# Modulation columns in pairs of chunks, two row tiles by 1024 columns to a slot

## The reference

```python
c_act = jax.nn.silu(c)
for l in range(DEPTH):                       # DEPTH = 2
    mod = c_act @ w_mod[l] + b_mod[l]        # w_mod[l]: 2048 x 6144
    shift, scale, gate = jnp.split(mod, 3, axis=-1)
    h = rmsnorm(x, norm_gain[l]) * (1.0 + scale[:, None, :]) + shift[:, None, :]
    proj = h @ w_in[l]                       # 2048 x 7504
    ...                                      # attention, retention, gates -> y_a, y_b
    y = jnp.concatenate([y_a, y_b], axis=-1) @ w_out[l]
    x = x + gate[:, None, :] * y
```

## Time and profile before

| | |
|---|---|
| median of three runs | 1870.87 us (1869.70 to 1872.94) |
| profiled execution | 1869.93 us |
| its span | 1868.1 us, 25006 instructions |
| TensorE busy | 1826.4 us (98%), granted clock 0.993 |
| VectorE busy | 1351.8 us (72%) |
| ScalarE busy | 990.8 us (53%) |
| split, L1859 | 721.1 us in 580 instructions |
| pieces, L1989 | 110.9 us in 154 and 52.3 us in 70 instructions |
| HBM read | 418.45 MB |

### The profile page before, as it was taken

One profiled execution on the slowest core, in us unless ns is written; L12 is line 12 of the kernel. 1 busy time (PEld: TensorE's weight loads), 2 busy tenths in 40 slices (PEclk: granted clock), 3 DMA queues, 4 the chain that ended last, 5 costly groups with the idle time before them and its releaser, 6 DMA issues.

```text
span 1868.1 us, 25006 instructions
## 1 busy us (share of the span) xinstructions
PE 1826.4 (98%) x9520; PEld 1512.4 (81%) x9520; DVE 1351.8 (72%) x1949; ACT 990.8 (53%) x1359; POOL 203.0 (11%) x256
## 2 busy tenths in 40 slices
PE   5989999999999999999999999999999999999997
PEld 3768788889888878888888888888888888888886
DVE  6979999988987778857765544488885466665555
ACT  6664455446447445544654644476765445444464
POOL 0000002100000000210000000044441020031001
PEclk9989999999999999999999999999999999999999
DMA  9989978965986986744365555554555555557562
GB/s 350 373 323 343 332 232 302 322 224 182 330 297 229 361 280 225 235 159 159 124 225 185 182 199 192 191 181 161 177 178 182 185 191 184 184 180 248 182 197 94
DMA packets 211826, 424.07 MB, mean 227 GB/s; under 512 B 7680, under 2 KB 12684, under 8 KB 210316
## 3 DMA queue, kind: packets, MB, share of 16 engines
q1 hardware_dynamic: 209788, 414.94, 65.6%
q10 hardware_dynamic: 1936, 7.76, 1.0%
HBM read 418.45 MB, written 4.21 MB: 226 GB/s over the span
## 4 chain that ended last, share of the span: by engine, by line
PE 91%; DMA 3%; DVE 2%; ACT 2%; issue 1%; SPq 0%; DVEq 0%; POOLq 0%; POOL 0%; ACTq 0%
PE acc L684 28%; PE acc L686 28%; PE acc L685 28%; DMA raw<-in_w_in 2%; DVE scr L2078 1%; DMA raw<-in_w_mod 1%; PE tps L725 1%; PE tps L765 1%; ACT w_hi L1418 0%; ACT proj L1393 0%; PE sps L996 0%; PE tps L988 0%; PE sps L952 0%; PE sps L893 0%; PE sps L892 0%
## 5 line engine op out<-in xcount | busy, mean ns | idle before, releaser
L1859 DVE TENSOR_TENSOR w_lo<-raw,w_hi 128x1024 fp32r<-128x1024 f32 (+1 forms) x580 | 721.1, 1249 | 444.8 <-ACT w_hi L1246 442.5
L1246 ACT ACTIVATE w_hi<-raw 128x1024 fp32r<-128x1024 f32 (+1 forms) x580 | 606.1, 1050 | 762.3 <-PE acc L686 684.3
L684 PE MATMUL acc<-w_hi,ht_hi 128*128 128x512 f32 (+1 forms) x2304 | 910.5, 395 | 0.5 <-issue 0.4
L686 PE MATMUL acc<-w_hi,ht_lo 128*128 128x512 f32 (+1 forms) x2304 | 894.2, 388 | 0.0
L685 PE MATMUL acc<-w_lo,ht_hi 128*128 128x512 f32 (+1 forms) x2304 | 892.3, 387 | 0.0
L686 PEld LDWEIGHTS acc<-w_hi,ht_lo 128*128 128x128 f32 x2304 | 432.4, 188 | 90.3
L684 PEld LDWEIGHTS acc<-w_hi,ht_hi 128*128 128x128 f32 x2304 | 432.9, 188 | 87.4 <-issue 3.2
L685 PEld LDWEIGHTS acc<-w_lo,ht_hi 128*128 128x128 f32 x2304 | 433.3, 188 | 83.4
L1989 DVE SCALAR_TENSOR_TENSOR scr<-raw,vcol,scr 128x512 f32<-128x512 f32 x154 | 110.9, 761 | 4.8 <-issue 0.4
L2078 DVE SCALAR_TENSOR_TENSOR scr<-raw,vcol,scr 128x1024 f32<-128x1024 f32 x56 | 68.0, 1278 | 6.6 <-DMA raw<-in_w_mod 6.6
L1989 DVE SCALAR_TENSOR_TENSOR proj<-raw,vcol,proj 128x512 f32<-128x512 f32 x70 | 52.3, 788 | 1.9
(11 more groups left out here) (305 smaller groups left out, 1446.8 us busy)
## 6 DMA issues: line engine op xcount, KB each, us to landing
raw<-in_w_in SPq DMA_DIRECT2D x208, 1024.0 KB, 5.1
raw<-in_w_mod SPq DMA_DIRECT2D x64, 1024.0 KB, 6.2
raw<-in_w_mod SPq DMA_DIRECT2D x64, 512.0 KB, 6.3
raw<-in_w_out SPq DMA_DIRECT2D x32, 1024.0 KB, 5.2
raw<-in_w_o SPq DMA_DIRECT2D x16, 1024.0 KB, 5.2
raw<-in_w_ple_gate SPq DMA_DIRECT2D x16, 1024.0 KB, 5.1
raw<-in_w_b_out SPq DMA_DIRECT2D x8, 1024.0 KB, 5.1
raw<-in_w_a_out SPq DMA_DIRECT2D x8, 1024.0 KB, 5.1
```

Source lines behind the costliest of these rows:

```text
L684: pe.matmul(o, hi_m, w_hi[:, slot, u, 0:width], start=start, stop=False)
L686: mm = pe.matmul(o, lo_m, w_hi[:, slot, u, 0:width], start=False, stop=stop)
L1246: act.activation(w_hi[:, x % SPL, :, 0:width], raw[:, j, 2 * (x % halves):2 * (x % halves) + 2, 0:width], ACT.Copy).then_inc(hi_ready, 1)
L1859: dve.tensor_tensor(w_lo[:, x % SPL, :, 0:width], raw[:, j, 2 * (x % halves):2 * (x % halves) + 2, 0:width], w_hi[:, x % SPL, :, 0:width]. ...
```

## The change

Behind the front, modulation chunks are made in pairs. A slot holds two row tiles by 1024 columns instead of four by 512, still 1 MB. A pair has eight pieces instead of two times four. Each piece is two instructions of 1024 columns into one accumulator of 1024; the closing addition is gone, and a wait and a semaphore increment of VectorE stand in its place. Both instructions of a piece now depend on the one before. TensorE adds up a pair in one group of eight narrow matmuls, and VectorE takes eight columns at once.

The pieces of layer 0 start one chunk later. The four of chunk 2 are gone; chunk 6 has four instead of two and chunk 7 has two (behind halves 5 and 7) where it had none. The other chunks keep their places. With this the gate's columns of layer 0 are complete later: their sum is behind half (6, 7) and their take behind the split of (7, 3). TensorE's turning of the gate's columns goes from (6, 4) to (7, 1), ScalarE's copy of them from half 8 to half 13 of chunks 6 and 7, and the DMA that writes them out from half 9 to half 14.

```diff
-PIECES = [{2: FULL, 3: FULL, 4: FULL, 5: FULL, 6: (1, 3), 8: (1, 3, 7), 9: FULL, 10: FULL, 11: (1, 3, 5),
+PIECES = [{3: FULL, 4: FULL, 5: FULL, 6: FULL, 7: (5, 7), 8: (1, 3, 7), 9: FULL, 10: FULL, 11: (1, 3, 5),
...
-                            mods[2 * j + 1] = piece // 4, piece % 4, item % RAW
+                            mods[2 * j + 1] = piece // 8, piece % 8, item % RAW
...
-                    if q == 3:
+                    if q == 7:
                         SUM_AT[n], TAKE_AT[n] = (l, k, 7), (l, k + 1, 3)
...
-            if 12 <= n < 16 or n == 23:
-                return macc_h[:, (n + n // 23) % 2, :, :]
-            return macc[:, n % 2, :, :]
+            return (macc_h if n in (6, 7, 11) else macc)[:, n % 2, :, :]
...
+            def land_pair(slot, src):
+                sp.wait_ge(raw_read, free.next(2))
+                sp.dma_start(raw[:, slot, :, :].rearrange("p (k a) n -> p k (a n)", a=2), src).then_inc(raw_landed[slot], 16)
...
-                            land(slot, full(wm[n // 12])(q, n % 12 * CH, CH))
+                            land_pair(slot, wm[n // 6][:, 2 * q:2 * q + 2, n % 6 * 2 * CH:(n % 6 + 1) * 2 * CH])
...
-            def mod_sums(src, parts=1):
+            def mod_sums(src):
                 pe.wait_ge(mod_taken, m_taken.next())
-                if parts == 1:
-                    pe.wait_ge(mod_ready, m_ready.next())
-                for j in range(4):
-                    for e in range(parts):
-                        mm = pe.matmul(tps[:, 1, j:j + 1], src[:, e, j * P:(j + 1) * P], ones,
-                                       start=e == 0, stop=e == parts - 1)
-                mm.then_inc(mod_summed, 1)
+                m_taken.skip(1)
+                pe.wait_ge(mod_ready, m_ready.next())
+                for e in range(2):
+                    for j in range(4):
+                        mm = pe.matmul(tps[:, 1, 4 * e + j:4 * e + j + 1], src[:, e, j * P:(j + 1) * P], ones,
+                                       start=True, stop=True)
+                mm.then_inc(mod_summed, 2)
...
-                if x == 4 and l == 0:
+                if x == 9 and l == 0:
                     gate_columns(l)
...
-            def mod_piece(to, q, slot, one_sum=False):
-
+            def mod_piece(n, q, slot):
+
+                to = home(n)
                 if q == 0:
-                    dve.wait_ge(mod_summed, m_free.next())
+                    dve.wait_ge(mod_summed, max(2 + 8, 2 * n))
                 dve.wait_ge(raw_landed[slot], m_land[slot].next(16))
                 for u in range(2):
-                    if q or u:
+                    src, c_col = raw[:, slot, 2 * u:2 * u + 2, :], v2("c", 2 * q + u)
+                    if q == 0 and u == 0:
+                        r = dve.tensor_scalar(to, src, c_col, None, ALU.mult)
+                    else:
                         dve.wait_ge(raw_read, own.ahead(0))
-                    for e in range(2):
...
+                        r = dve.scalar_tensor_tensor(to, src, c_col, to, ALU.mult, ALU.add)
                     r.then_inc(raw_read, 1)
                     own.skip(1)
-                if q == 3 and one_sum:
+                if q == 7:
                     dve.wait_ge(raw_read, own.ahead(0))
-                    dve.tensor_tensor(to[:, 0, :], to[:, 0, :], to[:, 1, :], ALU.add).then_inc(mod_ready, 1)
+                    dve.sem_inc(mod_ready, 1)
```

More of the change, by code:

```diff
@@ L87 @@
 FULL = (1, 3, 5, 7)
-PIECES = [{2: FULL, 3: FULL, 4: FULL, 5: FULL, 6: (1, 3), 8: (1, 3, 7), 9: FULL, 10: FULL, 11: (1, 3, 5),
+PIECES = [{3: FULL, 4: FULL, 5: FULL, 6: FULL, 7: (5, 7), 8: (1, 3, 7), 9: FULL, 10: FULL, 11: (1, 3, 5),
            12: (5, 7), 13: (3, 7), 15: (1, 3), 16: FULL, 17: FULL, 18: (1, 3)},
           {1: (3, 7), 2: (1, 3, 7), 3: (1, 3, 7), 4: (1, 5), 5: (1, 5), 6: (1, 3), 8: (1, 3)}]
+FRONT = 2
 RAW = 4
@@ L481, in slots_of_chunks @@
         def slots_of_chunks():
-            plan, item, piece = [{}, {}], 0, 4 * 8
+            plan, item, piece = [{}, {}], 0, 8 * 4
             for l in range(DEPTH):
-                for k in range(0 if l else 2, NCH + 5):
+                for k in range(0 if l else FRONT, NCH + 5):
                     rows, mods = [], {}
@@ L491, in slots_of_chunks @@
                         if 2 * j + 1 in PIECES[l].get(k, ()):
-                            mods[2 * j + 1] = piece // 4, piece % 4, item % RAW
+                            mods[2 * j + 1] = piece // 8, piece % 8, item % RAW
                             item, piece = item + 1, piece + 1
                     plan[l][k] = rows, mods
-                assert item % RAW == 0 and piece % 4 == 0
+                assert item % RAW == 0 and piece % 8 == 0
             return plan
@@ L1527, in norms @@
                         index_relu()
+                    if x == 13 and l == 0:
+                        gate_columns()
                     if x == 4 or x == 13:
@@ L1533, in norms @@
                                        ACT.Sqrt, bias=eps, scale=1.0 / HD).then_inc(root_ready, 1)
-                    if x == 8 and l == 0:
-                        gate_columns()
                     if x == 9:
-                        if l == 0:
-                            gates_out(l)
                         act.wait_ge(acc_taken, first_acc + 5)
@@ L1541, in norms @@
                     if x == 14:
+                        if l == 0:
+                            gates_out(l)
                         act.wait_ge(k_turned, ktn.next())
@@ L1873, in body @@
                             n, q, slot = mods[x % 8]
-                            mod_piece(home(n), q, slot, one_sum=True)
+                            mod_piece(n, q, slot)
                         if evac and x % group == min(3, group - 1) and not (first and x < group):
@@ L1974, in _, with mod_take @@
             own = Seen(dve, raw_read, 8)
-            def mod_piece(to, q, slot, one_sum=False):
+            def mod_piece(n, q, slot):
+                to = home(n)
                 if q == 0:
-                    dve.wait_ge(mod_summed, m_free.next())
+                    dve.wait_ge(mod_summed, max(2 + 8, 2 * n))
                 dve.wait_ge(raw_landed[slot], m_land[slot].next(16))
                 for u in range(2):
-                    if q or u:
+                    src, c_col = raw[:, slot, 2 * u:2 * u + 2, :], v2("c", 2 * q + u)
+                    if q == 0 and u == 0:
+                        r = dve.tensor_scalar(to, src, c_col, None, ALU.mult)
+                    else:
                         dve.wait_ge(raw_read, own.ahead(0))
-                    for e in range(2):
[L1985 to L1990, removed]
+                        r = dve.scalar_tensor_tensor(to, src, c_col, to, ALU.mult, ALU.add)
                     r.then_inc(raw_read, 1)
                     own.skip(1)
-                if q == 3 and one_sum:
+                if q == 7:
                     dve.wait_ge(raw_read, own.ahead(0))
-                    dve.tensor_tensor(to[:, 0, :], to[:, 0, :], to[:, 1, :], ALU.add).then_inc(mod_ready, 1)
[L1997 to L2001, removed]
+                    dve.sem_inc(mod_ready, 1)
+            def mod_take(n):
+                dve.wait_ge(mod_summed, m_sum.next(2))
+                dve.tensor_tensor(modc[:, 8 * n:8 * n + 8], tps[:, 1, 0:8], vcol[:, V1["b_mod"][0] + 8 * n:V1["b_mod"][0] + 8 * n + 8],
+                                  ALU.add).then_inc(mod_taken, 2)
             root, accs = Seen(dve, root_ready), Seen(dve, acc_taken, 2)
@@ L2141, in gains_of_second @@
                 if x == 1:
-                    mod_take(19)
+                    mod_take(9)
                     gains_of_layer(1)
```

## The result

| | before | after |
|---|---|---|
| median (range, runs) | 1870.66 us (1869.70 to 1872.94, 6) | 1877.61 us (1877.11 to 1878.41, 6) |
| profiled execution, span | 1869.93, 1868.1 us | 1877.11, 1875.1 us |
| VectorE busy, instructions | 1351.8 us, 1949 | 1329.6 us, 1797 |

The ratio is 1.0036, its 95% interval 1.0023 to 1.0049. The change is slower by 6.95 us; the forecast was +5.4, and 1876.3 us.

What follows compares the result with a forecast made beforehand. TensorE, busy 98%, was taken as the bound, with VectorE's w_lo delivery critical at (7, 6). Terms 5.3 + 1.0 - 0.9 = +5.4 us gave 1875.3 profiled, 1876.3 median; range 1871.0 to 1881.0.

Steps and rivals of the forecast that it cites:

- The bound and its place: TensorE bounds; VectorE's work matters only through timely w_lo halves, and the split of (7, 6) has no margin.
- The chain: VectorE's unbroken work from split (5, 7) to split (7, 6) in layer 0 grows by 6.4 us.
- rival B: Chain gives way: both 1.32 us ScalarE round trips vanish, pieces at lower bound; about 1872 us, chance 0.25.
- The start of the chain: At half (5, 7): one double group replaces three single groups ahead of it, so it comes 1.1 us earlier.
- The waits: TensorE waits at (7, 0), (7, 6) and the gate columns' turning, 5 to 7 us together, nothing elsewhere.
- It is the same lateness, called in earlier: TensorE's wait at the gate columns' turning, (7, 1), 2 to 2.5 us, adds nothing to the sum.
- Rival C: Waits in chunk 7 drop TensorE's clock to half rate, 1.4 us a time; 1879 to 1881 us, chance 0.10.
- A: The forecast itself: the chain is as summed; 1876.3 us, own range 1873.5 to 1879, chance 0.60.
- Rival D: Faster: without chunk 2's pieces the front's last wait, 5.3 us, shrinks; 1862 or 1869.6 us, chance 0.05.
- (8, 0): Behind (7, 6), the new piece at (7, 7) runs beside GpSimd and delays this half's split; +1.0 us, bounds 0 and 2.4.
- Behind the chain twelve groups become six doubles: -0.9: TensorE's sums after the chain: a double costs 1.75 us against 1.90 for two singles, saving 0.9 us.
- DMA: at nothing: Extra loads in chunks 6 and 7 cost nothing, since data moves there at 0.66 of the engines' time.

Runs made afterwards that it cites:

- load_in_7: Kernel before plus five useless VectorE fills (1.84 us) behind half (7, 4) of layer 0; 1872.25 us against 1870.35.
- load_in_4: Kernel before plus the same five useless VectorE fills, but behind half (4, 2) of layer 0; 1871.57 us against 1870.35.
- gate_take_early: Changed kernel with VectorE's take of the gate's last sums behind the split of (7, 1) instead of (7, 3); 1879.09 us.
- wide_old_places: Changed kernel's wide pieces and double sums, with layer 0's pieces and the gate's steps where they were before the change; 1869.87 us against 1870.56.
- no_pieces_in_7: Changed kernel with the two pieces of chunk 7 moved to (8, 5) and (11, 7); 1875.27 us.
- relief: wide_old_places without pieces in chunks 6 and 7 of layer 0, layer 1's chunk 6 pieces moved to chunk 5; 1869.07 us, repeated 1869.19.
- take_early_no_7: Changed kernel with both the gate's take at (7, 1) and chunk 7's pieces moved to (8, 5) and (11, 7); 1874.48 us.
- narrow_new_places: Kernel before with its old 512-column form, but pieces and gate steps at the change's new places; 1880.19 us against 1870.56.

## Why the prediction was right, and where it was off

**The bound and its place: right.** I had read that VectorE delivers the split of (7, 6) with no margin. load_in_7 shows it. I had read no other place. The index scores of chunk 4 have 2.3 us in hand, which late weights and fills together used up (load_in_4); the waits and stage sums that I had read show neither number.

**The chain: +6.94 measured, +6.4 forecast.** From the start of split (5, 7) to that of (7, 6) were 50.21 us; now they are 57.15. The timeline of VectorE in the changed kernel (start, duration):
```profile
229.89 1.23 DVE L1862 TENSOR_TENSOR w_lo<-raw,w_hi 128x1024 fp32r<-128x1024 f32 x1 [0.36 <-ACT w_hi L1249]
231.22 2.60 DVE L1991 SCALAR_TENSOR_TENSOR scr<-raw,vcol,scr 128x1024 f32<-128x1024 f32 x2
233.74 1.22 DVE L1862 TENSOR_TENSOR w_lo<-raw,w_hi 128x1024 fp32r<-128x1024 f32 x1
...
236.42 1.23 DVE L1862 TENSOR_TENSOR w_lo<-raw,w_hi 128x1024 fp32r<-128x1024 f32 x1
...
240.27 1.22 DVE L1862 TENSOR_TENSOR w_lo<-raw,w_hi 128x1024 fp32r<-128x1024 f32 x1
...
243.13 1.23 DVE L1862 TENSOR_TENSOR w_lo<-raw,w_hi 128x1024 fp32r<-128x1024 f32 x1
...
247.18 1.22 DVE L1862 TENSOR_TENSOR w_lo<-raw,w_hi 128x1024 fp32r<-128x1024 f32 x1
...
253.03 1.23 DVE L1862 TENSOR_TENSOR w_lo<-raw,w_hi 128x1024 fp32r<-128x1024 f32 x1 [1.32 <-ACT w_hi L1249]
...
258.39 1.22 DVE L1862 TENSOR_TENSOR w_lo<-raw,w_hi 128x1024 fp32r<-128x1024 f32 x1
...
260.96 1.22 DVE L1862 TENSOR_TENSOR w_lo<-raw,w_hi 128x1024 fp32r<-128x1024 f32 x1
...
266.48 1.22 DVE L1862 TENSOR_TENSOR w_lo<-raw,w_hi 128x1024 fp32r<-128x1024 f32 x1
...
279.70 1.22 DVE L1862 TENSOR_TENSOR w_lo<-raw,w_hi 128x1024 fp32r<-128x1024 f32 x1
...
287.04 1.22 DVE L1862 TENSOR_TENSOR w_lo<-raw,w_hi 128x1024 fp32r<-128x1024 f32 x1 [1.32 <-ACT w_hi L1249]
```
- A piece is 2.60 us listed, 2.52 to the next start (231.22 to 233.74); forecast 2.50. Split and piece are 3.85 (229.89 to 233.74); forecast 3.83.
- Half (6, 1) takes 3.85 (236.42 to 240.27), forecast 3.83. Half (6, 3) takes 4.05 (243.13 to 247.18), forecast 3.83: its piece is 0.2 longer.
- Half (6, 5) takes 5.36 (253.03 to 258.39), before 2.64: +2.72, forecast 2.6. Half (6, 7) takes 5.52 (260.96 to 266.48), before 2.58: +2.94, forecast 2.7. Half (7, 5) takes 7.34 (279.70 to 287.04), before 5.40: +1.94, forecast 1.98.
- Both round trips of 1.32 us to ScalarE are still there, so rival B, which needed them to vanish, did not happen.

The start of the chain is 1.75 us earlier (229.89 against 231.64). Of that the sums are 1.02, the offset's way from (2, 0) to (5, 0), forecast 1.1; 0.74 is the front's spread. So +6.94 - 1.75 = +5.2 for the split, and +5.30 for TensorE at (7, 6), forecast +5.3. That this is met to a tenth owes something to the spread: without it (7, 6) would stand at +6.0, and the misses of the chain's terms, 0.5 in all, would show. VectorE's work as a whole was sized less well, at some 30 us less where the busy time fell by 22: the instructions of a piece took 1313 and 1338 ns on the mean instead of 1276. No term of the sum used it.

The Trainium skill, "VectorE: DVE Perf Modes", section "The DRAIN you can't avoid", has it that a semaphore between chained instructions costs nothing extra; by it the chain would have grown 0.7 us less than forecast. The trace bears out the row instead: two instructions of 1.28 us are listed with 2.60 us together, so the waiting one starts 0.04 us behind the first one's end, and the split behind them, which need not wait, starts at 233.74, 0.08 us before their end.

**The waits: right in sum, not in place.** Forecast were 5 to 7 us between 255 and 300 us; measured are 5.0. I had the first at (7, 0) with 1.5 to 2.5; it is 0.76 there, and 1.53 already at (6, 6), where I had worked out no lead. The turning of the gate waits 2.00 us, forecast 2 to 2.5. "It is the same lateness, called in earlier" was half right: the wait is, but the slow matmuls behind it (+1.69) are not. That they cost only 0.1 us in the end, because the chain would have held TensorE at (7, 6) anyway, is luck. Rival C, the clock, was thus real; it lay in the cover of A, and in gate_take_early, where it lay outside it, it cost 2.38. Rival D, that the front's last wait shrinks without the pieces of chunk 2, did not happen: the wait is 5.1 us in the changed kernel, 5.1 in wide_old_places, which has those pieces, and was 5.3.

**(8, 0): right.** Forecast +1.0; the step is +0.90. The changed kernel, VectorE and GpSimd:
```profile
289.68 3.41 DVE L1991 SCALAR_TENSOR_TENSOR proj<-raw,vcol,proj 128x1024 f32<-128x1024 f32 x2
...
293.01 3.59 DVE L1862 TENSOR_TENSOR w_lo<-raw,w_hi 128x1024 fp32r<-128x1024 f32 x2
```
```profile
288.89 1.16 POOL L2644 TENSOR_TENSOR xn<-proj,st 128x256 f32 x1 [7.02 <-DVE st L2195]
290.02 1.99 POOL L2647 TENSOR_TENSOR scr<-scr,proj 128x384 f32<-128x384 f32 x1
...
293.53 1.99 POOL L2647 TENSOR_TENSOR scr<-scr,proj 128x384 f32<-128x384 f32 x1
```
In the kernel before, the first of GpSimd's two:
```profile
284.82 2.00 POOL L2646 TENSOR_TENSOR scr<-scr,proj 128x384 f32<-128x384 f32 x1
```
And TensorE in the changed kernel:
```profile
294.80 0.47 PE L687 MATMUL acc<-w_hi,ht_hi 128*128 128x512 f32 x1 [0.74 <-DVE w_lo L1862]
```
Beside GpSimd the piece takes 3.41 us instead of 2.60, and two splits 3.59 instead of 2.45; I had put 3.6 and 3.2. no_pieces_in_7 has no step at (8, 0), so it is this piece. GpSimd's 128x384 took 1.99 us twice, beside 2.00 and 1.46 before: it was lengthened already when VectorE had only splits there.

The Trainium skill, "SBUF — State Buffer", section "SBUF: two separate sides", describes the port pair as an exclusive lock held for the whole instruction. That both sides lengthen agrees with it; no run here tells a lock from a slower shared port.

**The step that failed: "Behind the chain twelve groups become six doubles: -0.9".** From +6.39 at (8, 3) the offset goes to +6.98, not to +5.5. This is the whole of the miss of 1.5 us (6.95 against 5.4). With the front's -0.74 taken out the change costs 7.7 us (last column of the table), 2.3 more than forecast, and the terms of the chain, 0.5, make up most of the rest. First, its size. A double group, TensorE in the changed kernel:
```profile
213.06 0.39 PE L689 MATMUL acc<-w_hi,ht_lo 128*128 128x512 f32 x1
213.28 1.84 PE L768 MATMUL tps<-kst,scr 128*128 128x1 f32 x16
214.98 0.49 PE L687 MATMUL acc<-w_hi,ht_hi 128*128 128x512 f32 x1
```
By the prediction's own working it is 214.98 - 213.06 - 0.23 = 1.69, and 0.15 on the next twelve matmuls: 1.84, where I had 1.75 by passes of 0.10 us. Two single groups are 1.90, so a pair saves 0.06, not 0.15. The offsets show it: -0.95 where the first single is gone, +0.89 to +0.90 where the double stands, six times, which makes -0.3.

Second, a wait that I had ruled out ("nothing elsewhere"). In layer 1, TensorE and VectorE in the changed kernel, then VectorE before:
```profile
766.20 0.50 PE L687 MATMUL acc<-w_hi,ht_hi 128*128 128x512 f32 x1 [0.49 <-DVE w_lo L1862]
```
```profile
764.92 1.23 DVE L1862 TENSOR_TENSOR w_lo<-raw,w_hi 128x1024 fp32r<-128x1024 f32 x1 [1.32 <-ACT w_hi L1249]
```
```profile
758.71 1.22 DVE L1859 TENSOR_TENSOR w_lo<-raw,w_hi 128x1024 fp32r<-128x1024 f32 x1 [1.32 <-ACT w_hi L1246]
```
This is the split of (7, 6) of layer 1, behind the same round trip. Before, it ended at 759.93 and TensorE came at 760.42, with 0.49 us to spare. Now a single group ahead of it is gone and its sums are made in a double behind the place, at (9, 1); TensorE comes 0.95 us earlier relative to the kernel's pace, and waits. The offset steps by 0.65 and 0.14 there, so most of what the missing group had given is taken back, while the double costs its 0.90 all the same. wide_old_places has the same wait, 0.5 us, and relief, without pieces in that chunk, has none. Together: -0.3 by the sums and +0.8 by the wait, and 0.16 at the very end whose cause I did not look for.

I had asked of the double sums only what TensorE saves, not what TensorE's lateness had been hiding.

**DMA: at nothing, not tested by itself.** Chunks 6 and 7 move data at 0.72 of the engines' time, 243 GB/s, up from 0.66 and 217; no wait of TensorE or VectorE in them is put down to a DMA.

## What to carry to other kernels

Work can be moved off or onto an engine only with its lead in hand, half by half: when a buffer is ready against when it is used. A busy share of 90% and a list without waits look the same with 2 us of lead and with none; a comparison of when a buffer is ready with when it is used tells them apart, and a few added fills of known length show which it is, if nothing else was late in that execution. And an operation that makes the bounding engine late may be what hides another's lateness: when it gets cheaper or moves, look at the next handover behind it.

## What the runs showed of the chip that I had not expected

- **The clock after a short wait is not told by its length alone.** Waits of 2.00 us (the change), 1.98 (no_pieces_in_7) and 3.44 us (gate_take_early) were followed, some at once and some three matmuls later, by matmuls 0.43 us apart, and cost 1.69, 1.69 and 2.38 us more. A wait of 1.97 us (load_in_7) was followed at once by the full rhythm of 0.23, and so was one of 1.55 (take_early_no_7), while in narrow_new_places a wait of 1.55, with one of 0.58 and eight narrow passes just ahead of it, was followed by matmuls 0.43 us apart (granted clock 0.51 from 269.20 to 272.70 us) and cost 1.69 more. Ahead of the 1.97 of load_in_7 TensorE had no wait from 143 us on; ahead of the 2.00 and 1.98 stood waits of 1.5 and 0.8 us, 16 and 8 us before. The 1.55 of take_early_no_7 had two such waits ahead of it as well, 18 and 27 us before.
- **A narrow pass costs nearly half of a wide matmul.** Sixteen passes of 128x1 take 1.84 us, 0.11 each, beside 0.227 for 128x512. Grouping them saves 0.06 us a pair of groups and no more.
